# Dot products of 2048 columns in one VectorE instruction instead of two, in a hybrid decoder layer

## The reference

```python
def peer_ffn(h, w_query, sub_keys, expert_u, expert_v):
    q = (h @ w_query).reshape(B, S, PEER_HEADS, 2, PEER_HALF)
    scores = jnp.einsum('bshcd,hckd->bshck', q, sub_keys)
    s_top, i_top = lax.top_k(scores, PEER_TOPK)
    ...
    best, pos = lax.top_k(cand, PEER_TOPK)
    expert_idx = jnp.take_along_axis(cand_idx, pos, axis=-1)
    gate = jax.nn.softmax(best, axis=-1)
    ...
        u = jnp.take(expert_u, ic, axis=0)
        act = jax.nn.gelu(jnp.einsum('ckd,cd->ck', u, xc), approximate=False)
        vv = jnp.take(expert_v, ic, axis=0)
        return jnp.einsum('ck,ckd->cd', gc * act, vv)
```

## Time and profile before

| | before |
|---|---|
| median of 3 runs | 2085.85 us (2084.48 to 2088.15) |
| the profiled execution | 2083.5 us, span 2081.4 us |
| VectorE busy | 1399.7 us (67%), 2242 instructions |
| GpSimd busy | 1008.5 us (48%) |
| TensorE busy | 1741.8 us (84%), mean granted clock 0.935 |
| gathers (software queue) | 465.64 MB, 55.0% of 16 engines' span |
| most that DMA moved in a slice of 52 us | 420 GB/s |

### The profile page before, as it was taken

One profiled execution on the slowest core, in us unless ns is written; L12 is line 12 of the kernel. 1 busy time (PEld: TensorE's weight loads), 2 busy tenths in 40 slices (PEclk: granted clock), 3 DMA queues, 4 the chain that ended last, 5 costly groups with the idle time before them and its releaser, 6 DMA issues.

```text
span 2081.4 us, 20985 instructions
## 1 busy us (share of the span) xinstructions
PE 1741.8 (84%) x7411; PEld 1172.5 (56%) x7411; DVE 1399.7 (67%) x2242; ACT 444.1 (21%) x719; POOL 1008.5 (48%) x643
## 2 busy tenths in 40 slices
PE   7999999999999999466655668777878899879965
PEld 7998799888998898422222224333334543334432
DVE  4328443223334347899888889999889877878777
ACT  5335253345433510101111101111011110000001
POOL 4444143444332413456665545545456756658751
PEclk9999799999999999878999889999889999999988
DMA  8996164655544589899999999999999989999996
GB/s 204 239 193 165 43 195 158 195 190 183 173 150 161 184 297 407 306 415 420 420 419 420 419 414 386 408 402 407 397 419 417 393 322 414 371 389 368 414 408 274
DMA packets 156492, 653.60 MB, mean 314 GB/s; under 512 B 23976, under 2 KB 29168, under 8 KB 93680
## 3 DMA queue, kind: packets, MB, share of 16 engines
q0 software_dynamic: 73728, 465.64, 55.0%
q1 hardware_dynamic: 82672, 186.77, 28.6%
HBM read 721.52 MB, written 2.10 MB: 348 GB/s over the span
## 4 chain that ended last, share of the span: by engine, by line
PE 46%; DMA 22%; DVE 16%; issue 7%; POOL 7%; ACT 1%; DVEq 0%; SPq 0%; POOLq 0%; ACTq 0%
DMA u_ring<-in_peer_u_dram,idx 10%; PE misc L1596 9%; PE acc L1307 5%; PE acc L1309 5%; PE acc L1308 5%; DVE product L1189 5%; PE acc L1315 5%; PE acc L1314 5%; PE acc L1316 5%; DVE product L1191 5%; DMA v_last<-in_peer_v_dram,idx 4%; DMA v_more<-in_peer_v_dram,idx 3%; DMA u_mid<-in_peer_u_dram,idx 2%; POOL v_low L486 2%; PE acc L1623 2%
## 5 line engine op out<-in xcount | busy, mean ns | idle before, releaser
L439 POOL TENSOR_TENSOR w_lo<-raw,w_hi 128x1024 fp32r<-128x1024 f32 x112 | 272.8, 2437 | 444.7 <-ACT w_hi L527 444.3
L1596 PE MATMUL misc<-v_low,diag 128*128 128x512 f32 x512 | 265.1, 670 | 136.1 <-ACT diag L700 85.2
L1596 PE MATMUL misc<-v_high,diag 128*128 128x512 f32 x512 | 267.3, 674 | 108.3 <-DMA v_high<-in_peer_v_dram,idx 72.5
L803 DVE TENSOR_TENSOR w_lo<-raw,w_hi 128x1024 fp32r<-128x1024 f32 x112 | 149.0, 1330 | 299.0 <-ACT w_hi L527 298.8
L527 ACT ACTIVATE w_hi<-raw 128x1024 fp32r<-128x1024 f32 x224 | 236.9, 1060 | 337.1 <-PE acc L1316 151.2
L479 POOL DMA_INDIRECT u_ring<-in_peer_u_dram,idx x160 | 209.6, 1310 | 201.7 <-DVE dots L1191 140.2
L1596 PEld LDWEIGHTS misc<-v_low,diag 128*128 128x128 f32 x512 | 105.8, 214 | 282.5 <-issue 203.8
L1307 PE MATMUL acc<-t_hi,w_hi 128*128 128x256 f32 x896 | 255.8, 286 | 0.2 <-issue 0.2
L1309 PE MATMUL acc<-t_hi,w_lo 128*128 128x256 f32 x896 | 254.1, 284 | 0.0
L1308 PE MATMUL acc<-t_lo,w_hi 128*128 128x256 f32 x896 | 254.0, 284 | 0.0
L1596 PEld LDWEIGHTS misc<-v_high,diag 128*128 128x128 f32 x512 | 106.0, 215 | 257.2 <-issue 156.4
(11 more groups left out here) (247 smaller groups left out, 2528.1 us busy)
## 6 DMA issues: line engine op xcount, KB each, us to landing
u_ring<-in_peer_v_dram SPq DMA_DIRECT2D x40, 1024.0 KB, 9.0
raw<-in_w_in_dram SPq DMA_DIRECT2D x64, 512.0 KB, 6.4
raw<-in_xattn_wk_dram SPq DMA_DIRECT2D x32, 512.0 KB, 4.7
raw<-in_xattn_wv_dram SPq DMA_DIRECT2D x32, 512.0 KB, 3.8
raw<-in_w_out_dram SPq DMA_DIRECT2D x32, 512.0 KB, 4.6
raw<-in_xattn_wq_dram SPq DMA_DIRECT2D x32, 512.0 KB, 4.4
raw<-in_xattn_wo_dram SPq DMA_DIRECT2D x32, 512.0 KB, 4.8
praw<-in_peer_wq_dram SPq DMA_DIRECT2D x32, 512.0 KB, 9.4
```

What stands on the lines that cost most here:

```text
L439: nc.gpsimd.tensor_tensor(w_lo[:, j % RING, :, :], raw[:, j % RING, :, :], w_hi[:, j % RING, :, :].bitcast(F32), ALU.subtract).then_inc(lo ...
L1596: ins = nc.tensor.matmul(o, diag[:, n % 4, :], v_slot(n % VS)[:, i * CW:(i + 1) * CW], start=False, stop=False)
```

## The change

Each dot is one instruction over all 2048 columns. `dots` loses the dimension of the halves, and `sum_dots`, `dot_sums` and the semaphore `dots_summed` go. `gelu` reads `dots` and waits until the 16th dot of its group is done.

```diff
-    dots = put("dots", [P, 2, 2, TOP], F32)
-    dot_sums = put("dot_sums", [P, 2, TOP], F32)
+    dots = put("dots", [P, 2, TOP], F32)
...
-                act.wait_ge(dots_summed, g + 1)
-                nc.scalar.activation(acts[:, q, :], dot_sums[:, q, :], ACT.Gelu, scale=rstd[:, c:c + 1]).then_inc(gelu_done, 1)
+                act.wait_ge(dot_done, g * TOP + TOP)
+                nc.scalar.activation(acts[:, q, :], dots[:, q, :], ACT.Gelu, scale=rstd[:, c:c + 1]).then_inc(gelu_done, 1)
...
-            def sum_dots(g, q):
-
-                dve.wait_ge(dot_done, g * TOP + TOP)
-                nc.vector.tensor_tensor(dot_sums[:, q, :], dots[:, q, 0, :], dots[:, q, 1, :], ALU.add).then_inc(dots_summed, 1)
-
...
-                    nc.vector.tensor_tensor_reduce(out=product[:, 0:D // 2], in0=u_slot(n)[:, 0:D // 2], in1=hn[:, c, 0:D // 2], scale=1.0, scalar=0.0,
-                                                   op0=ALU.mult, op1=ALU.add, accum_out=dots[:, q, 0, k:k + 1])
-                    nc.vector.tensor_tensor_reduce(out=product[:, D // 2:], in0=u_slot(n)[:, D // 2:], in1=hn[:, c, D // 2:], scale=1.0, scalar=0.0,
-                                                   op0=ALU.mult, op1=ALU.add, accum_out=dots[:, q, 1, k:k + 1]).then_inc(dot_done, 1)
+                    nc.vector.tensor_tensor_reduce(out=product[:, :], in0=u_slot(n), in1=hn[:, c, :], scale=1.0, scalar=0.0,
+                                                   op0=ALU.mult, op1=ALU.add, accum_out=dots[:, q, k:k + 1]).then_inc(dot_done, 1)
...
-                sum_dots(g, q)
```

More of the change, by code:

```diff
@@ L249, in hybrid_layer @@
         routed, nbest_ready, gexp_done = sem("routed"), sem("nbest_ready"), sem("gexp_done")
-        dots_summed, lists_done, hot_ready, wT_done, wT_copied, tile_used = sem("dots_summed"), sem("lists_done"), sem("hot_ready"), sem("wT_done"), sem("wT_copied"), sem("tile_used")
+        lists_done, hot_ready, wT_done, wT_copied, tile_used = sem("lists_done"), sem("hot_ready"), sem("wT_done"), sem("wT_copied"), sem("tile_used")
         dot_done, gelu_done, wts_ready, diag_ready, v_used = sem("dot_done"), sem("gelu_done"), sem("wts_ready"), sem("diag_ready"), sem("v_used")
@@ L1259, in _ @@
             dot_products(0, 0, 0, range(8, TOP))
-            sum_dots(0, 0)
             gates(1)
@@ L1268, in _ @@
             dot_products(1, 1, 0, range(AHEAD, TOP))
-            sum_dots(1, 1)
             route(3)
```

## The result

The change makes the kernel slightly slower. The median goes from 2083.76 us (20 runs, 2080.25 to 2088.57) to 2088.74 us (20 runs, 2084.04 to 2092.78). The medians differ by 5.0 us. The ratio, which is estimated from all the runs and isn't the quotient of the medians (that would be 1.0024), is 1.0027 with an interval of 1.002 to 1.0034, or 5.6 us. The prediction was 2092 us against a median of 2085.85 us, or +6.15 us on it, with "slower" as the likeliest sign.

What follows compares the result with a forecast made beforehand. It took bytes to bind 880 to 1213 us, near-full DMA to 1577, then TensorE to 1699. Terms 2.5 + 0 + 4 + 0 = +6.5 us on the profiled 2083.5 gave 2090, 2092 us as median; range 2077 to 2108.

Steps and rivals of the forecast that it cites:

- VectorE's dots: Dots on VectorE: one instruction drops an accumulator read, 2.45 us from dot to dot instead of 2.53, 20 us gained.
- The shorter dots are worth nothing: Periods 2 to 7, 880 to 1213 us: bytes bind, so shorter dots turn into waits for u; 0 taken.
- The hold on GpSimd: Gathers on GpSimd: one issued 0.12 us into a long dot stands until its end, 2.98 us, 1.07 us more.
- Group 1, +2.5 us: Group 1, 827 to 880 us: slower issues lengthen the lap of four dots from 11.27 to 12.2 us; bounds -1 and +4.
- Periods 2 to 7, 0 us taken: 880 to 1213 us: bytes bind and slower issues come out of the queue; 0 us, bounds -1.6 and +5.
- The queue runs thin in the nine dots between two routing steps: Periods 2 to 7: the case behind the upper bound of +5 us, the DMA queue running thin there.
- Periods 8 to 13, +4 us taken: 1213 to 1577 us: later gather issues lengthen the lap, partly absorbed by queue standing; +4 us, bounds -8 and +14.
- the net of +14 us of the lap: Periods 8 to 13: three issues cost +2.7 us, four dots return 0.33; +2.3 us a lap, 14 us for six.
- The prediction's 13 us: 1213 to 1577 us: the most anybody can win there, by raising 405 GB/s to 420.
- faster: Rival: GpSimd's waits for TensorE absorb slower issues in group 1 and periods 8 to 13; 2078 us, chance 0.22.
- no difference: Rival: gain becomes waiting for u, slower issues stand less in the queue; 2086 to 2088 us, chance 0.30.
- The far slower one: Rival: GpSimd becomes the bound in later periods, 62 us a period with 10 us of waits; 2109 us, chance 0.12.

Runs made afterwards that it cites:

- one_input_long: Changed kernel with each dot a reduction over 2048 columns of u alone, product with the token left out: 2076.79 us, 0.9969 of the kernel before.
- one_input_halves: Kernel before with each half dot a reduction over 1024 columns of u alone, product with the token left out: 2076.43 us, ratio 0.9967.
- long_3_15: Kernel before with long dots in groups 3 to 15, halves kept in groups 0 to 2: ratio 1.001 to the kernel before.
- psum_long: Changed kernel with the dots of groups 2 to 7 reading the token from PSUM: 2087.41 us, 1.0019 of the kernel before.
- the no-v runs: Changed kernel and kernel before, each without 124 of 128 v gathers: 2043.43 us (0.981) with long dots, 2050.86 us (0.9838) with halves.
- long_0_2: Kernel before with long dots in groups 0 to 2, halves kept in groups 3 to 15: ratio 1.0009 to the kernel before.
- gate6_halves: Kernel before with ScalarE's gate_exp moved behind the seventh diagonal of a period instead of the fourth: 2082.23 us, ratio 0.9997.

## Why the prediction was nearly right

**VectorE's dots: right.** A pitch of 2.45 us was forecast, 2.44 measured; the instruction takes 2292 ns. VectorE is busy 22 us less (20 forecast, and the sums of the halves on top).

**The shorter dots are worth nothing: right.** The bytes were to turn the gain of groups 2 to 7 into waits for u. From 880 to 1213 us the changed kernel's VectorE waits 18.1, 9.4 and 7.1 us for the three kinds of slot, 35 us in all, where it was 21. `one_input_long` and `one_input_halves`, whose dots differ by 0.06 us, have the same time over the whole kernel, to some 2 us.

**The hold on GpSimd: right.** 2.98 us was forecast for a gather 0.12 us into a dot, 3.01 measured; one gather for each dot; GpSimd well above 1008 us.

**Group 1, +2.5 us: wrong in sign.** The lap of 12.2 us took 6.68 us for the transfer, as 8.59 less its issue. The changed kernel's gather from 830.15 to 832.28 is landed when the dot at 836.93 starts, 4.65 us later. The 6.68 us had held time in the queue. Issued one by one at a slower pace, transfers stand less: the same reasoning that I applied to the later periods and left out here. It is a reading of the two traces; no run varied the pace alone. From first to twelfth dot it took 29.25 us (826.73 to 855.98), where 30.0 before and 33.6 in the sum. Group 1 became 1.5 us shorter, and this isn't chance of one trace: from the first dot of group 1 to that of group 2 five kernels with long dots there take 61.5 to 62.4 us, five with halves 62.0 to 63.9, on average 1.2 us more.

**Periods 2 to 7, 0 us taken: too small, inside the bound of +5.** The rate fell to 387, 389 and 403 GB/s in three stretches between 900 and 960 us where it had been 413 to 418, and the traces put 2.9 us on the way from group 2 to group 8. "The queue runs thin in the nine dots between two routing steps" was named as a bound and weighed too lightly, for group 2. For the groups behind it 0 was right: `long_3_15` takes 323.7 us from group 2 to group 8, the kernel before 323.8. `psum_long` returns 1.7 us of the 2.9.

**Periods 8 to 13, +4 us taken: about +2 in the traces, which is within what two traces may differ by.** Here the net of +14 us of the lap had been cut to a third. The waits for TensorE took up more of it: 126.5 us fell to 35. The prediction's 13 us as all that could be won there came from the bytes alone; the no-v runs show a second limit, the handover, which keeps a group at 58 us with only 295 GB/s.

The terms of +2.5, 0 and +4 were measured at -1.5 for group 1 and, less certainly, +3 and +2 in the traces; behind 1577 us 0 was forecast and the traces differ by about as much as two executions may. The forecast sum of +6.5 stands beside +5.0 (5.6 by the ratio). That it came so close is in part luck: the error in group 1 and that in periods 2 to 7 have opposite signs. `long_0_2` also shows that the traces' gain up to group 2 isn't one in the end. The rivals "faster" and "no difference" gave GpSimd's waits as the place where the loss would vanish: they took up most of it, but not all. The far slower one, GpSimd as the bound, would have needed GpSimd without waits from 1213 us on, and it kept 35 us of them.

Open is where exactly the last 3 us lie, by which the median of the changed kernel exceeds its own traced execution, and why `gate6_halves` loses in groups 14 and 15 what it gains before them. That the loss as a whole hangs on the hold rests on the pair of `one_input` kernels, which leave out a part of the work; with the dot kept whole the hold was taken away in groups 2 to 7 alone, where little of the loss lies.

## What to carry to other kernels

Before joining two VectorE instructions into one, look at whether GpSimd issues gathers beside them. If both inputs are in SBUF, a gather stands until the instruction ends, and the saving per instruction (0.08 us here) is set against as much as 1.1 us for each gather (3.01 against 1.91). Where an instruction must be long, moving one operand to PSUM frees GpSimd at no cost in the instruction (2.29 us either way here), if there is room in PSUM; in this kernel it brought no time that could be measured. A transfer's time in a chain of waits can hold time in the queue (4.65 us here where 6.68 were counted on); if the change alters when it is issued, that part must not be carried over as a constant.

## What was not expected of the hardware

- Taking the second input away saves 6.6 us in the kernel before already, more than the 5.0 us that joining the dots adds.
- The input's place decides, not the length. The same instruction of 2048 columns takes 2.29 us with its token in SBUF or in PSUM, and a gather beside it 3.01 us or 0.95 us.
- A gather ends 0.81 to 0.82 us after the VectorE instruction that held it, for 512, 1024 and 2048 columns alike (1.39, 1.91 and 3.01 us, each begun about 0.1 us into it). Nearly its whole 0.94 us is left to do when it is let go.
